# Gate spread of a sparse-expert layer: column one-hots eight tokens at a time on VectorE, gated rows divided over three engines

## Chip, cores and metric

The kernel runs on one core of one Trainium2 chip. The metric is the device time of one execution in microseconds (us); lower is better. TensorE (PE in the profile, with its weight loads as PEld), VectorE (DVE), ScalarE (ACT), GpSimd (POOL) and the DMA queue of SyncE (SP) run their own instruction streams and meet at semaphores.

## The reference, cut to what matters

The whole program is a two-direction gated linear attention mixer, a PEER layer and two further transformer layers over 512 tokens of width 1024. The change is in the PEER layer. Each token picks 128 experts (8 heads with 16 picks each) out of 128 x 128, and gives each a gate:

```python
expert = (jnp.take_along_axis(i1, top_c // PEER_TOPK, axis=-1) * PEER_N_KEYS
          + jnp.take_along_axis(i2, top_c % PEER_TOPK, axis=-1))
gate = jax.nn.softmax(top_s, axis=-1)
act = jax.nn.gelu(jnp.einsum("pd,ped->pe", xb, jnp.take(u, eb, axis=0)), approximate=False)
return jnp.einsum("pe,ped->pd", (gb * act).astype(v.dtype), jnp.take(v, eb, axis=0))
```

## The kernel before, in words

For 384 of the 512 tokens (`TD`) the kernel does not gather expert rows. It computes all 16384 experts for those tokens as dense products and multiplies by a gate matrix that is zero where an expert was not picked. (The other 128 tokens do gather their rows, later.) So each token needs a 128 x 128 matrix of gates: expert number = 128 * e1 + e2, and the gate of pick s belongs at column e2[s] and row e1[s]. The stage that makes these matrices is called the spread, and it is the only place that the change touches.

At its start the tiles `e1T`, `e2T` and `gT` (the profile calls all of them `eT`) hold e1, e2 and the gate with the 128 picks on the partitions and the 384 tokens along the free axis. `iota` is 0 to 127 along the free axis. For token t two 128 x 128 f32 tiles are made:

- `ob`: a one-hot row per pick, `iota == e2T[:, t]` (the column one-hot);
- `oa`: `(iota == e1T[:, t]) * gT[:, t]` (the gated row).

TensorE multiplies the two (L2199, two passes in f32, so 768 matmul records for 384 tokens), four tokens to a PSUM bank. ScalarE copies each full bank to `stage` (L2223, 96 copies), and after 32 tokens the DMA queue of SyncE writes a stage to `gd` in DRAM (L2257, 12 writes).

Who makes what: VectorE makes all 384 `oa` tiles (L2235) and 72 of the `ob` tiles (L2238). GpSimd makes 192 `ob` tiles with one comparison each (L2249). ScalarE makes the remaining 120 `ob` tiles with two instructions each, `|e2 - iota|` (L2215) and `relu(1 - x)` (L2217). `expert_engine(t)` fixes who makes `ob` of token t, with a period of 16 tokens: 3 on VectorE, 5 on ScalarE, 8 on GpSimd.

There are 16 buffers of each kind (`NOH`), so whoever makes a tile for token t waits for the matmul of token t - 16. Each engine goes through its own tokens in order. ScalarE's order of tiles and bank copies is `spread_order`: its tiles of tokens 4q + 8 to 4q + 11 come before the copy of bank q. The stage begins when the transposed picks have been copied out of PSUM (L2091), and the next stage (the experts) starts after all five engines have left this one.

Of the kernel before, what the change touches and what calls it, by code (L numbers as in the profile page):

```python
# [7 lines left out]
ALU = mybir.AluOpType  # L8
ACT = mybir.ActivationFunctionType
# [1668 lines left out]
TD = 384  # L1678
# [29 lines left out]
def peer_plan(k):  # L1708
    m = k.m
    k.U2 = m.pair("Up", [128, KC, TX])  # L1710
    k.own = Net()
    k.own.x = m.sb("ownx", [128, D])
    k.own.at, k.own.atf = m.sb("ownat", [128, NSLOT], U32), m.sb("ownatf", [128, NSLOT])
    k.own.gate, k.own.dot, k.own.w = (m.sb("own", [128, NSLOT]) for _ in range(3))
    own_u = m.top
    k.early = [m.sb("early", [128, 4, TD // 2]) for _ in range(5)]
    k.early += [k.X[:, c:c + 4, TX:TX + TD // 2] for c in (0, 4)]
    m.top = own_u
    k.own.u = [m.sb("ownu", [128, D]) for _ in range(NUB)]
    top = m.top  # L1720
    m.top = own_u + 10 * D
    k.n2 = NormMod(k, "n2", k.X, k.sc2, k.MOD[0][:, 24:32, :], k.U2, (XR,), sums_at=own_u, sums=4, rows=3)
    assert m.top <= top and k.n2.s.end <= own_u + 10 * D
    m.top = top
    k.peer_top = m.top
    k.iota, k.marks = m.sb("iota", [128, 128]), m.sb("marks", [128, 32])
    k.e1T, k.e2T, k.gT = (m.sb("eT", [128, TD]) for _ in range(3))
    top2 = m.top
    k.R = Retrieval(k)
    m.top = top2  # L1730
    k.oa = [m.sb("oa", [128, 128]) for _ in range(NOH)]
    k.ob = [m.sb("ob", [128, 128]) for _ in range(NOH)]
    k.stage = [m.sb("stage", [128, 128, BT]) for _ in range(2)]
    last = m.sb("early", [128, 4, TD // 2])
    assert k.R.end <= m.top
    k.early += [m.sb("early", [128, 4, TD // 2]) for _ in range(NE - 8)] + [last]
    m.top = top
    k.gt = [m.sb("gt", [128, TD // BT, 4, BT]) for _ in range(2)]
    k.acts = [m.pair("act", [128, 2, TD]) for _ in range(2)]
    k.ge = [m.sb("ge", [128, TD]) for _ in range(2)]  # L1740
    k.own.acc = k.X[:, 0:4, TX:T]
    side = m.top
    k.side = [m.sb("side", [128, TW]) for _ in range(2)]
    k.cb2 = m.sb("cb", [128, 2 * D])
    k.dots3 = Dots(k, "experts", k.cb2, k.X[:, 4:8, TX:T])
    k.own.v = [m.sb("ownv", [128, D]) for _ in range(NVB)]
    end, m.top = m.top, side
    k.ot = [m.sb("ot", [128, D]) for _ in range(3)]
    m.top = end
# [94 lines left out]
def early_pe(k, n):  # L1844

    u = view(take(k, ("u", n)), KC)
    for i in range(2):
        project(k, k.B[EARLY_BANKS[n] + i][:, 0:TD], u, KC, 128 * i, k.U2, DENSE).then_inc(
            *k.pe.inc("mm", ("u", n, i), *([("tile", u.j)] if i else [])))
# [310 lines left out]

def expert_engine(t):

    if t % 16 in (1, 5, 7, 11, 13):
        return "act"
    return "dve" if t % 16 in (3, 8, 14) else "pool"


NOH = 16  # L2170


def spread_order():

    out = [("hot", t) for t in range(8)]
    for q in range(TD // 4):
        if q + 2 < TD // 4:
            out += [("hot", t) for t in range(4 * q + 8, 4 * q + 12)]
        out.append(("group", q))
    return out  # L2180


def spread_pe(k):
    pe = k.pe
    for q in range(TD // 4):
        b = k.B[q % 8]
        pe.wait_ge("early", (8, 1))
        if q >= 8:
            pe.wait_ge("staged", q - 8)
        for i in range(4):  # L2190
            t = 4 * q + i
            pe.wait_ge("hot_a", t)
            if expert_engine(t) == "act":
                pe.wait_ge("hot_act", t)
            elif expert_engine(t) == "dve":
                pe.wait_ge("hot_dve", t)
            else:
                pe.wait_ge("hot_pool", t)
            ins = pe.e.matmul(b[:, i * 128:(i + 1) * 128], k.ob[t % NOH][:], k.oa[t % NOH][:], start=True, stop=True)  # L2199
            ins.then_inc(*pe.inc("mm", ("hot", t)))  # L2200
    pe.mark("spread")
    pe.wait_ge("staged", TD // 4 - 7)
    early_pe(k, NE - 1)


def spread_act(k):
    a = k.act
    a.after("retrieve", "pe", "dve", "pool")
    for what, t in spread_order():
        if what == "hot":  # L2210
            if expert_engine(t) == "act":
                ob = k.ob[t % NOH]
                if t >= NOH:
                    a.wait_ge("mm", ("hot", t - NOH))
                a.e.activation(ob[:], k.iota[:], ACT.Abs, bias=k.e2T[:, t:t + 1], scale=-1.0).then_inc(*a.inc("hot_act", (t, 0)))  # L2215
                a.wait_ge("hot_act", (t, 0))
                a.e.activation(ob[:], ob[:], ACT.Relu, bias=k.one[:, 0:1], scale=-1.0).then_inc(*a.inc("hot_act", t))  # L2217
        else:
            n, i0 = 4 * t // BT, 4 * t % BT
            a.wait_ge("mm", ("hot", 4 * t + 3))  # L2220
            if n >= 2:
                a.wait_ge(f"stored{n % 2}", n - 2)
            a.e.activation(k.stage[n % 2][:, :, i0:i0 + 4], k.B[t % 8].rearrange("p (t i) -> p i t", t=4), ACT.Copy).then_inc(  # L2223
                *a.inc("staged", t))
    a.mark("spread")


def spread_dve(k):
    v = k.dve
    v.after("retrieve", "pe", "act", "pool")  # L2230
    v.wait_ge("chosen", ("T", 2))
    for t in range(TD):
        if t >= NOH:
            v.wait_ge("mm", ("hot", t - NOH))
        v.e.tensor_scalar(k.oa[t % NOH][:], k.iota[:], k.e1T[:, t:t + 1], k.gT[:, t:t + 1], ALU.is_equal, ALU.mult).then_inc(  # L2235
            *v.inc("hot_a", t))
        if expert_engine(t) == "dve":
            v.e.tensor_scalar(k.ob[t % NOH][:], k.iota[:], k.e2T[:, t:t + 1], None, ALU.is_equal).then_inc(*v.inc("hot_dve", t))  # L2238
    v.mark("spread")


def spread_pool(k):
    g = k.pool
    g.after("retrieve", "pe", "act", "dve")
    for t in range(TD):
        if expert_engine(t) == "pool":
            if t >= NOH:
                g.wait_ge("mm", ("hot", t - NOH))
            g.e.tensor_scalar(k.ob[t % NOH][:], k.iota[:], k.e2T[:, t:t + 1], None, ALU.is_equal).then_inc(*g.inc("hot_pool", t))  # L2249
    g.mark("spread")  # L2250


# [1885 lines left out]
def tensor_program(k):  # L4138
# [9 lines left out]
    n2_pe(k)  # L4148
    retrieve_pe(k)
    spread_pe(k)  # L4150
    experts_pe(k)
    join_pe(k)
# [18 lines left out]
def scalar_program(k):  # L4171
# [8 lines left out]
    n2_act(k)  # L4180
    retrieve_act(k)
    spread_act(k)
    experts_act(k)
    join_act(k)
# [19 lines left out]
def vector_program(k):  # L4204
# [8 lines left out]
    n2_dve(k)  # L4213
    retrieve_dve(k)
    spread_dve(k)
    experts_dve(k)
    join_dve(k)
# [19 lines left out]
def gpsimd_program(k):  # L4237
# [9 lines left out]
    n2_pool(k)  # L4247
    retrieve_pool(k)
    spread_pool(k)
    experts_pool(k)  # L4250
    join_pool(k)
# [34 lines left out]
def make_plan(k):  # L4286
# [32 lines left out]
    assert m.top <= heads  # L4319
    m.top = base  # L4320
    peer_plan(k)
    m.top = base
    k.r64, k.r96 = m.sb("r64", [128, 128]), m.sb("r96", [128, 128])
# [247 lines left out]
```

## Time and profile before

| what | value |
|---|---|
| timed runs, median | 5397.58 us (5397.45 to 5402.66, 3 runs) |
| span of the profiled execution | 5393.7 us |
| spread stage, first `oa` to last write of a stage issued | 1306.8 to 1441.3 us of that span |
| busy over the span: PE, DVE, ACT, POOL | 91%, 57%, 36%, 22% |

The profiled execution is one run of its own; its span lies 3.9 us below the median of the timed runs, within what a time includes around the span. The busy shares are means over all stages, so they say little on this one: in the spread all four engines are busy most of the time, and the rest of the kernel is mostly TensorE's.

### The profile page before, as it was taken

Reading aid. Unit: us, or ns where it says so; the run is one execution under the profiler, and the core shown is the slowest. Engines: PE = TensorE matmul, PEld = TensorE weight load, DVE = VectorE, ACT = ScalarE, POOL = GpSimd, SP = SyncE. Lnnn points to the kernel's source line nnn. Section 1 sums busy time; section 2 is a strip of 40 time slices with the busy share of each in tenths; the row PEclk is TensorE's granted clock in tenths of the full one; section 3 lists DMA queues with packets and bytes.
Section 4 is the critical chain, followed back from the end, with each engine's and each line's share of the span. In section 5 each row is a group of like instructions: output and inputs, shape, how many; then the busy total and the mean of one; then the engine's idle time right before and its main releaser. Section 6 shows DMA issues by size and latency. Waiting matters only on the chain.

```text
span 5393.7 us, 67249 instructions
## 1 busy us (share of the span) xinstructions
PE 4930.6 (91%) x27217; PEld 4138.9 (77%) x27217; DVE 3101.0 (57%) x5380; ACT 1915.5 (36%) x2842; POOL 1206.4 (22%) x1009
## 2 busy tenths in 40 slices
PE   7998989998899999999799898989999799889999
PEld 7887877787688888887668786778888577667787
DVE  5444455589667777776442535356656534554555
ACT  3445522235733323333342424322222343343333
POOL 1111100046644555442120002100000120021000
PEclk8999989999999999999899999999999899999999
DMA  4111023422578898984101010122322101112221
GB/s 153 52 56 57 31 94 121 155 86 108 211 251 295 313 310 310 310 291 163 51 20 64 16 47 30 48 86 110 114 97 104 43 32 64 36 45 94 86 94 71
DMA packets 157155, 636.29 MB, mean 118 GB/s; under 512 B 12352, under 2 KB 62544, under 8 KB 106288
## 3 DMA queue, kind: packets, MB, share of 16 engines
q1 hardware_dynamic: 112528, 467.97, 24.5%
q0 software_dynamic: 42240, 160.88, 8.4%
q8 instruction: 217, 3.56, 0.3%
q10 hardware_dynamic: 2080, 3.15, 0.2%
q14 instruction: 90, 0.74, 0.0%
HBM read 595.25 MB, written 36.70 MB: 117 GB/s over the span
## 4 chain that ended last, share of the span: by engine, by line
PE 74%; DVE 13%; ACT 7%; issue 3%; POOL 2%; DMA 2%; DVEq 0%; ACTq 0%; POOLq 0%; SPq 0%
PE banks L261 61%; PE banks L2918 2%; PE banks L3017 1%; PE banks L2923 1%; DVE cols L2949 1%; DVE oa L2235 1%; ACT P L2967 1%; PE banks L3044 1%; PE banks L990 1%; DVE raw L527 1%; DVE prod L527 1%; PE banks L335 1%; DMA X<-ctxT_in 1%; ACT spl1H L192 1%; PE banks L382 1%
## 5 line engine op out<-in xcount | busy, mean ns | idle before, releaser
L261 PE MATMUL banks<-UH,spl1H 128*128 128x512 f32 (+1 forms) x1600 | 588.4, 368 | 37.8 <-DVE spl1L L210 9.2
L210 DVE TENSOR_TENSOR spl0L<-raw,spl0H 128x2048 fp32r<-128x2048 f32 (+2 forms) x170 | 372.9, 2193 | 401.1 <-ACT spl0H L192 372.0
L210 DVE TENSOR_TENSOR spl1L<-raw,spl1H 128x2048 fp32r<-128x2048 f32 (+2 forms) x163 | 366.3, 2247 | 405.6 <-ACT spl1H L192 380.7
L261 PE MATMUL banks<-UL,spl1H 128*128 128x512 f32 (+1 forms) x1600 | 581.6, 364 | 0.0
L261 PE MATMUL banks<-UH,spl1L 128*128 128x512 f32 (+1 forms) x1600 | 581.3, 363 | 0.0
L261 PE MATMUL banks<-UH,spl0H 128*128 128x512 f32 (+2 forms) x1184 | 432.6, 365 | 37.8 <-DVE UL L480 10.4
L192 ACT ACTIVATE spl1H<-raw 128x2048 fp32r<-128x2048 f32 (+1 forms) x170 | 313.2, 1842 | 333.7 <-PE banks L261 255.7
L192 ACT ACTIVATE spl0H<-raw 128x2048 fp32r<-128x2048 f32 (+3 forms) x171 | 306.2, 1791 | 343.5 <-PE banks L261 254.8
L261 PE MATMUL banks<-UL,spl0H 128*128 128x512 f32 (+2 forms) x1184 | 427.2, 361 | 0.0
L261 PE MATMUL banks<-UH,spl0L 128*128 128x512 f32 (+2 forms) x1184 | 426.9, 361 | 0.0
L261 PEld LDWEIGHTS banks<-UH,spl1H 128*128 128x128 f32 x1600 | 304.5, 190 | 97.5 <-issue 36.6
L261 PE MATMUL banks<-UpH,spl0H 128*128 128x384 f32 (+1 forms) x1008 | 348.9, 346 | 26.6 <-issue 21.3
L261 PE MATMUL banks<-UpL,spl0H 128*128 128x384 f32 (+1 forms) x1008 | 345.6, 343 | 0.0
L261 PE MATMUL banks<-UpH,spl0L 128*128 128x384 f32 (+1 forms) x1008 | 345.5, 343 | 0.0
L261 PEld LDWEIGHTS banks<-UH,spl1L 128*128 128x128 f32 x1600 | 304.6, 190 | 51.0
L261 PEld LDWEIGHTS banks<-UL,spl1H 128*128 128x128 f32 x1600 | 304.8, 191 | 50.1 <-issue 0.5
L261 PE MATMUL banks<-spl1H,actH 128*128 128x512 f32 x708 | 282.4, 399 | 50.0 <-issue 40.1
L2949 DVE TENSOR_REDUCE cols<-banks 128x1 f32<-128x768 f32 (+3 forms) x240 | 190.7, 795 | 189.6 <-PE banks L2923 106.0
L261 PEld LDWEIGHTS banks<-UH,spl0H 128*128 128x128 f32 (+1 forms) x1184 | 225.3, 190 | 83.5 <-issue 35.5
L261 PE MATMUL banks<-spl1L,actH 128*128 128x512 f32 x708 | 280.1, 396 | 0.0
L261 PE MATMUL banks<-spl1H,actL 128*128 128x512 f32 x708 | 279.8, 395 | 0.0
L4095 POOL TENSOR_TENSOR cv<-cv 128x768 f32<-128x768 f32 (+1 forms) x44 | 68.9, 1566 | 846.6 <-DVE cv L4061 846.6
(483 smaller groups left out, 11698.6 us busy)
## 6 DMA issues: line engine op xcount, KB each, us to landing
raw<-uT_in SPq DMA_DIRECT2D x64, 1024.0 KB
raw<-ev_in SPq DMA_DIRECT2D x64, 1024.0 KB
raw<-up_in SPq DMA_DIRECT2D x44, 1024.0 KB
raw<-ada_in SPq DMA_DIRECT2D x40, 1024.0 KB
gd<-stage SPq DMA_DIRECT2D x12, 2048.0 KB, 6.8
gt<-gd SPq DMA_DIRECT2D x32, 768.0 KB, 7.5
side<-ada_in SPq DMA_DIRECT2D x24, 1024.0 KB, 7.0
raw<-gate_in SPq DMA_DIRECT2D x24, 1024.0 KB
```

Source lines behind the costliest of these rows:

```text
L192: a.e.activation(k.spl[i % SPL].h[:, 0:w], k.raw[j % RAW][:, 0:w], ACT.Copy).then_inc(*a.inc("w_hi", j))
L210: v.e.tensor_tensor(s.l[:, 0:w], k.raw[j % RAW][:, 0:w], s.h[:, 0:w].bitcast(F32), ALU.subtract).then_inc(*v.inc("w_lo", j))
L261: ins = pe.e.matmul(out, x, y, start=start and i == 0 and j == 0, stop=stop and i == n - 1 and j == 2)
L335: ins = pe.e.matmul(s.sums[:, o:o + 1], s.sq[i % len(s.sq)][:, c * 128:(c + 1) * 128], k.ones[:, 0:1], start=(i == 0 and c == 0), stop=(j ...
L382: ins = pe.e.matmul(b[:, c * 128:(c + 1) * 128], k.ones[:], d[:, c, :], start=True, stop=True)
L527: v.e.scalar_tensor_tensor(x if r else S.out, x, 1.0, w, ALU.mult, ALU.mult, accum_out=MOD[:, 2 * t + c, r:r + 1]).then_inc(*v.inc("dot", ...
L990: ins = pe.e.matmul(o[:, c * 64:(c + 1) * 64], w.S[:, c, x * 128:(x + 1) * 128], w.qd[:, c * 64:(c + 1) * 64], start=False, stop=(c == ord ...
L2235: v.e.tensor_scalar(k.oa[t % NOH][:], k.iota[:], k.e1T[:, t:t + 1], k.gT[:, t:t + 1], ALU.is_equal, ALU.mult).then_inc(*v.inc("hot_a", t))
L2918: ins = pe.e.matmul(k.W[1 + j][:, at:at + n], Q[lo:hi, q * 128:(q + 1) * 128], K[lo:hi, k0:k0 + n], start=True, stop=True)
L2923: ins = pe.e.matmul(k.W[1 + jj][:, at:at + n], Q[lo:hi, q * 128:(q + 1) * 128], K[lo:hi, k0:k0 + n], start=True, stop=True)
L2949: v.e.reduce_max(mx, src, AX_X).then_inc(*v.inc("largest", (tag, i, j)))
L4095: g.e.tensor_tensor(va[:, 0:w], va[:, 0:w], ga[:, 0:w], ALU.mult).then_inc(*g.inc("ffn_prod", (l, j)))
```

## The change

The column one-hots `ob` are now all made on VectorE, for eight tokens (`OBT`) in one instruction: `iota` broadcast over eight tokens is compared with eight columns of `e2T` broadcast over 128. There are 48 of them, in 3 buffers of eight tokens each (`NOB`). Their first is made ahead of everything and then each one block ahead of its rows. The gated rows `oa`, which were all VectorE's, are divided by `row_engine(t)` with a period of 24 tokens: 3 on ScalarE (48 in all), 10 on GpSimd (160), 11 on VectorE (176). ScalarE's version of a gated row is `|e1 - iota|` and then `relu(gate - gate * x)`, for which it first makes the negated gates `ngT` out of PSUM. TensorE waits for the block of columns and for the row's engine; its matmuls, the bank copies and the stage writes stay.

```diff
@@ peer_plan
-    k.e1T, k.e2T, k.gT = (m.sb("eT", [128, TD]) for _ in range(3))
+    k.e1T, k.e2T, k.gT, k.ngT = (m.sb("eT", [128, TD]) for _ in range(4))
-    k.ob = [m.sb("ob", [128, 128]) for _ in range(NOH)]
+    k.ob = [m.sb("ob", [128, OBT, 128]) for _ in range(NOB)]
@@
-def expert_engine(t):
-
-    if t % 16 in (1, 5, 7, 11, 13):
-        return "act"
-    return "dve" if t % 16 in (3, 8, 14) else "pool"
-
-
-NOH = 16
+NOH = 16
+OBT = 8
+NOB = 3
+
+
+def row_engine(t):
+
+    if t % 8 == 3:
+        return "act"
+    return "pool" if t % 24 in (0, 2, 5, 7, 9, 12, 14, 16, 18, 21) else "dve"
@@ spread_act
+    a.e.activation(k.ngT[:], k.B[6][:, 0:TD], ACT.Copy, scale=-1.0).then_inc(*a.inc("hot_row_act", "minus"))
+    a.wait_ge("hot_row_act", "minus")
-                a.e.activation(ob[:], k.iota[:], ACT.Abs, bias=k.e2T[:, t:t + 1], scale=-1.0).then_inc(*a.inc("hot_act", (t, 0)))
-                a.wait_ge("hot_act", (t, 0))
-                a.e.activation(ob[:], ob[:], ACT.Relu, bias=k.one[:, 0:1], scale=-1.0).then_inc(*a.inc("hot_act", t))
+                a.e.activation(oa[:], k.iota[:], ACT.Abs, bias=k.e1T[:, t:t + 1], scale=-1.0).then_inc(*a.inc("hot_row_act", (t, 0)))
+                a.wait_ge("hot_row_act", (t, 0))
+                a.e.activation(oa[:], oa[:], ACT.Relu, bias=k.gT[:, t:t + 1], scale=k.ngT[:, t:t + 1]).then_inc(
+                    *a.inc("hot_row_act", t))
@@
+def hot_columns_dve(k, b):
+    v = k.dve
+    if b >= NOB:
+        v.wait_ge("mm", ("hot", OBT * (b - NOB) + OBT - 1))
+    e = k.e2T[:, b * OBT:(b + 1) * OBT].unsqueeze(2).to_broadcast([128, OBT, 128])
+    v.e.tensor_tensor(k.ob[b % NOB][:], k.iota[:].unsqueeze(1).to_broadcast([128, OBT, 128]), e, ALU.is_equal).then_inc(
+        *v.inc("hot_cols", b))
@@ spread_dve
+    hot_columns_dve(k, 0)
     for t in range(TD):
-        if t >= NOH:
-            v.wait_ge("mm", ("hot", t - NOH))
-        v.e.tensor_scalar(k.oa[t % NOH][:], k.iota[:], k.e1T[:, t:t + 1], k.gT[:, t:t + 1], ALU.is_equal, ALU.mult).then_inc(
-            *v.inc("hot_a", t))
-        if expert_engine(t) == "dve":
-            v.e.tensor_scalar(k.ob[t % NOH][:], k.iota[:], k.e2T[:, t:t + 1], None, ALU.is_equal).then_inc(*v.inc("hot_dve", t))
+        if t % OBT == 0 and t // OBT + 1 < TD // OBT:
+            hot_columns_dve(k, t // OBT + 1)
+        if row_engine(t) == "dve":
+            if t >= NOH:
+                v.wait_ge("mm", ("hot", t - NOH))
+            v.e.tensor_scalar(k.oa[t % NOH][:], k.iota[:], k.e1T[:, t:t + 1], k.gT[:, t:t + 1], ALU.is_equal, ALU.mult).then_inc(
+                *v.inc("hot_row_dve", t))
@@ spread_pool
-        if expert_engine(t) == "pool":
+        if row_engine(t) == "pool":
             if t >= NOH:
                 g.wait_ge("mm", ("hot", t - NOH))
-            g.e.tensor_scalar(k.ob[t % NOH][:], k.iota[:], k.e2T[:, t:t + 1], None, ALU.is_equal).then_inc(*g.inc("hot_pool", t))
+            g.e.tensor_scalar(k.oa[t % NOH][:], k.iota[:], k.e1T[:, t:t + 1], k.gT[:, t:t + 1], ALU.is_equal, ALU.mult).then_inc(
+                *g.inc("hot_row_pool", t))
```

VectorE at the start of the spread, before the change: after the three copies out of PSUM come runs of `oa` with an `ob` now and then.

```order
L2091 COPY eT<-banks 128x384 x3
L2235 TENSOR_SCALAR oa<-iota,eT 128x128 x4
L2238 TENSOR_SCALAR ob<-iota,eT 128x128
L2235 TENSOR_SCALAR oa<-iota,eT 128x128 x5
L2238 TENSOR_SCALAR ob<-iota,eT 128x128
L2235 TENSOR_SCALAR oa<-iota,eT 128x128 x6
```

The same place of the same engine with the change: two blocks of columns come first, then three or four rows between blocks.

```order
L2091 COPY eT<-banks 128x384 x3
L2238 TENSOR_TENSOR ob<-iota,eT 128x1024 x2
L2253 TENSOR_SCALAR oa<-iota,eT 128x128 x3
L2238 TENSOR_TENSOR ob<-iota,eT 128x1024
L2253 TENSOR_SCALAR oa<-iota,eT 128x128 x4
L2238 TENSOR_TENSOR ob<-iota,eT 128x1024
L2253 TENSOR_SCALAR oa<-iota,eT 128x128 x4
```

What moved on VectorE: 72 single comparisons and 208 of its 384 rows are gone, and 48 instructions of 1024 elements stand in their place.

ScalarE at the start of the spread, before the change.

```order
L2215 ACTIVATE ob<-iota,eT 128x128
L2217 ACTIVATE ob<-ob,one 128x128
L2215 ACTIVATE ob<-iota,eT 128x128
L2217 ACTIVATE ob<-ob,one 128x128
L2223 ACTIVATE stage<-banks 128x128x4
L2215 ACTIVATE ob<-iota,eT 128x128
L2217 ACTIVATE ob<-ob,one 128x128
L2223 ACTIVATE stage<-banks 128x128x4
```

The same place with the change: the negated gates first, then one pair for every two bank copies.

```order
L2211 ACTIVATE eT<-banks 128x384
L2219 ACTIVATE oa<-iota,eT 128x128
L2221 ACTIVATE oa<-oa,eT 128x128
L2219 ACTIVATE oa<-iota,eT 128x128
L2221 ACTIVATE oa<-oa,eT 128x128
L2228 ACTIVATE stage<-banks 128x128x4 x2
L2219 ACTIVATE oa<-iota,eT 128x128
L2221 ACTIVATE oa<-oa,eT 128x128
L2228 ACTIVATE stage<-banks 128x128x4 x2
```

What moved on ScalarE: 120 pairs became 48, and one copy of 384 elements stands ahead of its first row. On GpSimd nothing changes its place: 192 single comparisons become 160 comparisons with a multiplication, in one unbroken run.

## Rows read from the trace of the kernel before

**Rows 1.** The page: busy time of each engine over the span.

```profile
span 5393.7 us, 67249 instructions
PE 4930.6 (91%) x27217; PEld 4138.9 (77%) x27217; DVE 3101.0 (57%) x5380; ACT 1915.5 (36%) x2842; POOL 1206.4 (22%) x1009
```

**Rows 2.** Chain that ended last, 1306.8 to 1441.3 us: shares by engine and line.

```profile
by line: DVE oa L2235 53.2%; PE banks L2199 10.8%; ACT stage L2223 10.2%; ACT ob L2217 9.3%; DVE ob L2238 7.5%; ACT ob L2215 6.9%; DMA gd<-stage 4.6%; issue 2.0%
```

**Rows 3.** Three stretches of the spread: start:end, length, busy us of each engine (instructions).

```profile
1306.80:1354.00 47.20, 40.82 (x271) 35.20 (x271) 47.19 (x176) 45.29 (x118) 45.99 (x75) 0.94 0.32 135
1354.00:1435.50 81.50, 69.78 (x469) 58.00 (x470) 74.84 (x281) 79.13 (x206) 73.22 (x118) 1.00 0.47 196
1435.50:1441.30 5.80, 5.08 (x35) 4.43 (x36) 0.22 (x1) 5.55 (x15) 0.36 (x1) 1.00 0.38 161
```

**Rows 4.** Groups of instructions, 1306.8 to 1441.3 us: busy us, mean ns, idle before.

```profile
L2249 POOL TENSOR_SCALAR ob<-iota,eT 128x128 f32<-128x128 f32 x192 | 119.6, 639 | 15.6 <-PE banks L2199 8.4 <-DVE eT L2091 6.1
L2223 ACT ACTIVATE stage<-banks 128x512 f32<-128x512 f32 x96 | 55.5, 579 | 0.6 <-PE banks L2199 0.4
```

**Rows 5.** Timeline of ScalarE, 1358.3 to 1361.1 us: start, length, instruction.

```profile
1358.27 0.40 ACT L2217 ACTIVATE ob<-ob,one 128x128 f32<-128x128 f32 x1
1358.58 0.39 ACT L2215 ACTIVATE ob<-iota,eT 128x128 f32<-128x128 f32 x1
1359.00 0.40 ACT L2217 ACTIVATE ob<-ob,one 128x128 f32<-128x128 f32 x1
1359.31 0.58 ACT L2223 ACTIVATE stage<-banks 128x512 f32<-128x512 f32 x1
1359.78 0.39 ACT L2215 ACTIVATE ob<-iota,eT 128x128 f32<-128x128 f32 x1
```

**Rows 6.** Timeline of TensorE at 1340 us, and its L2199 with durations.

```profile
1340.15 0.72 PE L2199 MATMUL banks<-oa,ob 128*128 128x128 f32 x5
...
L2199 PE MATMUL banks<-oa,ob x768: 274/275/552, 1307.7 to 1440.4; 128*128 128x128 f32 x192
```

**Rows 7.** Timeline of VectorE, a 1024-element comparison (L2000) behind a 2048-element subtraction.

```profile
1163.04 2.28 DVE L210 TENSOR_TENSOR spl0L<-raw,spl0H 128x2048 fp32r<-128x2048 f32 x1
1165.23 1.22 DVE L2000 TENSOR_TENSOR ge<-small,marks 128x1024 f32<-128x1024 f32 x1
1166.37 0.87 DVE L1942 MAX8 vals<-sc 128x8 f32<-128x128 f32 x4
```

**Rows 8.** Timeline of GpSimd in those microseconds, and one undisturbed such instruction (groups, 1270 to 1275 us).

```profile
1163.30 3.31 POOL L2139 TENSOR_TENSOR cand<-vals 128x64 f32<-128x64 f32 x1 [0.83 <-DVE topc L1953]
...
L2139 POOL TENSOR_TENSOR cand<-vals 128x64 f32<-128x64 f32 x1 | 0.3, 302 | 0.8 <-DVE topc L1953 0.8
```

**Rows 9.** Timelines of GpSimd and VectorE at 1296 us: both start within 0.06 us.

```profile
1296.17 4.56 POOL L224 TENSOR_TENSOR spl0L<-raw,spl0H 128x2048 fp32r<-128x2048 f32 x1 [7.82 <-issue]
...
1296.23 5.58 DVE L2040 TENSOR_TENSOR eq<-eq,small 128x1024 f32<-128x1024 f32 x1
```

**Rows 10.** Timelines of GpSimd and VectorE in the spread, single instructions.

```profile
1309.41 0.71 POOL L2249 TENSOR_SCALAR ob<-iota,eT 128x128 f32<-128x128 f32 x1
1310.11 0.60 POOL L2249 TENSOR_SCALAR ob<-iota,eT 128x128 f32<-128x128 f32 x1
1310.68 0.60 POOL L2249 TENSOR_SCALAR ob<-iota,eT 128x128 f32<-128x128 f32 x1
...
1309.45 0.28 DVE L2238 TENSOR_SCALAR ob<-iota,eT 128x128 f32<-128x128 f32 x1
1309.90 0.33 DVE L2235 TENSOR_SCALAR oa<-iota,eT 128x128 f32<-128x128 f32 x1
1310.16 0.39 DVE L2235 TENSOR_SCALAR oa<-iota,eT 128x128 f32<-128x128 f32 x1
```

**Rows 11.** GpSimd scalar instructions elsewhere: durations (min/median/max ns), two operations (L1164), one (L873).

```profile
L1164 POOL TENSOR_SCALAR k<-lg x16: 833/838/842, 96.1 to 419.6; 128x768 f32<-128x768 f32 x16
L873 POOL TENSOR_SCALAR kd<-b x24: 922/926/929, 114.5 to 679.5; 128x256 f32<-128x256 f32 x24
```

More of the change, by code:

```diff
@@ L2191, in spread_pe @@
             t = 4 * q + i
[L2192 to L2196, printed above, removed]
-            else:
-                pe.wait_ge("hot_pool", t)
-            ins = pe.e.matmul(b[:, i * 128:(i + 1) * 128], k.ob[t % NOH][:], k.oa[t % NOH][:], start=True, stop=True)
+            pe.wait_ge("hot_cols", t // OBT)
+            if row_engine(t) == "act":
+                pe.wait_ge("hot_row_act", t)
+            elif row_engine(t) == "dve":
+                pe.wait_ge("hot_row_dve", t)
+            else:
+                pe.wait_ge("hot_row_pool", t)
+            ins = pe.e.matmul(b[:, i * 128:(i + 1) * 128], k.ob[t // OBT % NOB][:, t % OBT, :], k.oa[t % NOH][:], start=True, stop=True)
             ins.then_inc(*pe.inc("mm", ("hot", t)))
@@ L2208, in spread_act @@
     a.after("retrieve", "pe", "dve", "pool")
+    a.e.activation(k.ngT[:], k.B[6][:, 0:TD], ACT.Copy, scale=-1.0).then_inc(*a.inc("hot_row_act", "minus"))
+    a.wait_ge("hot_row_act", "minus")
     for what, t in spread_order():
         if what == "hot":
-            if expert_engine(t) == "act":
-                ob = k.ob[t % NOH]
+            if row_engine(t) == "act":
+                oa = k.oa[t % NOH]
                 if t >= NOH:
                     a.wait_ge("mm", ("hot", t - NOH))
-                a.e.activation(ob[:], k.iota[:], ACT.Abs, bias=k.e2T[:, t:t + 1], scale=-1.0).then_inc(*a.inc("hot_act", (t, 0)))
-                a.wait_ge("hot_act", (t, 0))
-                a.e.activation(ob[:], ob[:], ACT.Relu, bias=k.one[:, 0:1], scale=-1.0).then_inc(*a.inc("hot_act", t))
+                a.e.activation(oa[:], k.iota[:], ACT.Abs, bias=k.e1T[:, t:t + 1], scale=-1.0).then_inc(*a.inc("hot_row_act", (t, 0)))
+                a.wait_ge("hot_row_act", (t, 0))
+                a.e.activation(oa[:], oa[:], ACT.Relu, bias=k.gT[:, t:t + 1], scale=k.ngT[:, t:t + 1]).then_inc(
+                    *a.inc("hot_row_act", t))
         else:
```

## Prediction, made before the changed kernel ran

> **What bounds the kernel now.** I read the page first: TensorE is busy 91% of the span, GpSimd 22% [rows 1]. That mean says nothing on the spread, so I took the chain of the stage next. There TensorE has 11%; rows and columns made on VectorE have 61%, ScalarE's three lines 26% [rows 2]. The stage lasts 134.5 us and lies wholly on the chain.
>
> Busy time by stretch shows who sets the pace [rows 3]. Until 1354 us VectorE is busy 47.19 of 47.20 us. From then to 1435.5 us ScalarE is (79.13 of 81.50), VectorE has gaps (74.84), and for the last 5.8 us ScalarE finishes alone. ScalarE's own pace follows from its timeline [rows 5]: a pair takes 0.42 + 0.31 = 0.73 us from start to start, a bank copy 0.47. For 120 pairs and 96 copies that is 120 x 0.73 + 96 x 0.47 = 132.7 us, the length of the stage. VectorE runs 176 instructions in the first 47.2 us, 0.268 us each, so 456 of them need 122 us. GpSimd starts one in 47.20 / 75 = 0.63 us, 192 x 0.63 = 121 us; it is busy for 119.6 of the 134.5 us, and the 96 bank copies of ScalarE waited for TensorE 0.4 us in all [rows 4]. TensorE, when fed, needs (0.72 - 0.275) / 4 = 0.111 us per matmul record [rows 6], so 768 x 0.111 = 85.5 us: the floor of this stage. So three engines stand close together at 121 to 133 us, and the change can give up to 49 us, if no engine takes over the place of the slowest.
>
> **The change part by part.** ScalarE: 48 pairs and 96 copies, 48 x 0.73 + 96 x 0.47 = 80.2 us, plus one copy of 384 elements at the start, about 0.5 us. A scale read per partition in the second of a pair isn't in the trace; even 0.1 us more is 5 us of a slack of 50. ScalarE leaves the path.
>
> VectorE: 176 rows x 0.268 = 47.2 us. The 48 blocks of columns have a close relative in the trace: a comparison of 1024 elements with both inputs broadcast takes 1.22 us, 1.14 from its start to the next start [rows 7]. 48 x 1.14 = 54.7 us. Sum 101.9 us without waits, against 122 before.
>
> GpSimd: 160 instructions instead of 192. An undisturbed one takes 0.60 us and the next starts 0.57 to 0.58 after it [rows 10]; with fewer VectorE rows in its way I take 0.60 per row, 96 us in all. The new form has a second operation and a second value per partition. L1164 does two operations on 768 elements in 0.84 us, while L873, one operation with a value per partition, takes 0.93 us for 256 [rows 11]: the second operation is cheap, the value read per partition is what costs. Bounds for the second value: nothing, or the work per element once more. From 128 elements at 0.60 us and 256 at 0.926, an element costs 2.5 ns, so once more is 0.32 us, 51 us over 160 rows. I take nothing, since one tile of values more is not one pass more, and keep part of it as a rival.
>
> These three sums alone would give 102 us. But a price stands in the trace that the diff doesn't show: **VectorE instructions with two SBUF inputs and GpSimd instructions exclude each other.** At 1296 us a GpSimd subtraction starts 0.06 us ahead of a VectorE product of 1024 elements [rows 9]. GpSimd ends at 1300.73; VectorE's 1.22 us become 5.58 and end at 1301.81, 1.08 us after it. So VectorE asks 0.14 us after its start and then holds for 1.08. The other way round, GpSimd's 0.30 us instruction starts at 1163.30 inside a VectorE subtraction, and a broadcast comparison follows that until 1166.45. It ends at 1166.61, after 3.31 us [rows 7, 8]. It too asks some 0.14 us in. That comparison is of the form of the new columns, so broadcasting does not exempt them.
>
> The Trainium skill ("SBUF — State Buffer", section "Who interferes with whom") says the same: a VectorE instruction with two SBUF inputs contends with a GpSimd instruction that reads SBUF. It adds that whoever comes first keeps the port pair for its whole instruction. The pairs of rows above agree. In the spread it is otherwise for GpSimd's scalar form. Within one GpSimd instruction (1309.41, 0.71 us) one VectorE comparison starts at 1309.45 and takes 0.28, and the rows after it go on [rows 10]. One side pays 0.1 at most: GpSimd 0.71 instead of 0.60, or VectorE 0.39 instead of 0.33 at 1310.16. So that form keeps the other out for about 0.1 us of its 0.60, from 0.14 to 0.25 after its start (1310.16 + 0.14 + 0.06 is 0.25 after 1310.11).
>
> What does a block of columns then cost GpSimd? An instruction under way past its 0.25 us finishes; the next waits at its 0.14 until the hold of 1.08 ends. The delay is 1.08 less the time from VectorE's grant to GpSimd's next request. With GpSimd the slowest, VectorE waits in its queue for a matmul, and TensorE for GpSimd's row. Let a GpSimd row end at 0: the matmul pair ends near 0.49 (0.1 + 0.11 + 0.28), VectorE starts 0.04 later and is granted at 0.67, while GpSimd would ask at 0.70 and, another row on, at 1.28. The block's wait is on tokens 7, 15 and 23 of 24, which lie 0, 1 and 2 tokens (0.22 us each) behind the last GpSimd row. Grants at 0.67, 0.89 and 1.11 cost GpSimd 1.05, 0.69 and 0.91 us, mean 0.88. 48 x 0.88 = 42 us. Bounds: 0.6 (a grant just after GpSimd's window) and 1.08 (the whole hold each time), 29 to 52 us.
>
> **The sum.** GpSimd is the bound: 96 + 42 = 138 us, plus 1.2 us behind its last row (matmul 0.5, bank copy 0.6), 139.4 us against 134.5: +5 us. VectorE, with 102 us and some tenths of waiting per block, has room and hides in it; so do ScalarE (80) and TensorE (85.5). At the start TensorE gets its first pair about 1 us later than before, since the columns come first; that lies within GpSimd's sum, which counts its wait on the first block. Behind the stage all is as before: stage write, then the loads of the experts, and any shift goes through one to one. The span of 5393.7 becomes 5398.6, and as the median lay 3.9 us above the span, 5397.6 + 5 = **5402.5 us**. With the bounds of the delay (29 and 52 us for 42) it is 5389 to 5412.
>
> **The rivals.**
> (a) GpSimd isn't held up: its port need falls between VectorE's holds, or VectorE is the one that waits and briefly. For it: GpSimd's own window is short. Against: 3.31 us for 0.30 [rows 8]. VectorE then bounds, 101.9 plus 1.2 ahead of its first row and 1.2 behind the last, 104.5 us: 30 us less, 5368 us. If VectorE pays 0.3 us for each block, 14 us more, 5382. It decides once the delay per block is below 0.55 us: then GpSimd needs less than 123 us.
> (b) GpSimd keeps the pair for its whole instruction in this form too. Then the next one asks just behind VectorE's grant, each block costs the full 1.08, and 96 + 52 + 1.2 gives 149 us: +15, 5412 us. Against it stand the undisturbed VectorE rows of [rows 10]; for it, [rows 9]. The skill's rule named above is this case.
> (c) The second value per partition costs GpSimd 0.1 us a row (a third of the bound): +16 us on the forecast, 5418 us. It decides from 0.04 us a row, where it passes the band of no change.
> (d) The change does not relieve ScalarE, because its row instructions with a scale per partition take much longer. To matter they must rise by over 1 us each: no row speaks for it.
>
> **Chances.** The forecast's mechanism 0.46, with its own range 5389 to 5410; (a) 0.22; (b) 0.15; (c) 0.17; (d) under 0.01. A measurement of this kernel tells about 0.2% (10.8 us) from no change, so 5386.8 to 5408.4 is "same". Of the forecast's 0.46, 0.03 falls below that band and 0.03 above. (a) is faster. (b) and (c) are slower. Faster 0.25, same 0.40, slower 0.35. A range from 5368 to 5420 leaves out about half of (a) and half of (c), 0.2 in all.
>
> **What the new profile would show.** Right: GpSimd busy without a gap in the spread, with about 48 of its 160 rows lengthened to 1.2 to 1.7 us and the others at 0.60; VectorE's column blocks at 1.2 to 1.3 us and gaps before its rows that end with TensorE; ScalarE busy about 60% of the stage, with gaps. If (a), GpSimd's rows all stay near 0.6 and VectorE has no gaps, the stage takes 105 to 120 us. If (b), column blocks of 1.2 to 1.7 us and a stage near 149. If (c), the shortest GpSimd rows stand well above 0.60 us. The prediction is wrong if the chain of the stage goes through TensorE's own pace or ScalarE, neither of which I expect, or if what the stage gains is taken back by the loads that follow it.

## The result, and the profile after

The changed kernel takes 5435.4 us (median of 4 runs) against 5397.5 us: slower by 37.9 us, a ratio of 1.007 (95% interval 1.0058 to 1.0082). The forecast was 5402.5 us with a range up to 5420, so both the number and the range missed.

The chain of the spread stage after, shares by line (for [rows 2]):

```profile
by line: POOL oa L2265 76.6%; PE banks L2201 22.0%; DMA gd<-stage 4.0%; issue 1.0%; ACT stage L2228 0.3%
```

Three stretches of the stage (for [rows 3]): start:end, length, then busy us of PE, PEld, DVE, ACT and POOL with their instructions:

```profile
1306.00:1354.00 48.00, 33.62 (x201) 27.59 (x202) 30.51 (x63) 24.90 (x53) 47.99 (x43) 0.91 0.21 88
1354.00:1474.00 120.00, 86.94 (x536) 69.27 (x536) 74.35 (x162) 63.81 (x134) 120.00 (x113) 0.99 0.38 158
1474.00:1480.20 6.20, 5.94 (x39) 5.08 (x40) 0.49 (x2) 3.71 (x8) 4.52 (x6) 1.00 0.01 3
```

And the groups of the stage (for [rows 4]): busy us, mean ns, idle before and who ended it:

```profile
L2265 POOL TENSOR_SCALAR oa<-iota,eT 128x128 f32<-128x128 f32 x160 | 172.5, 1093 | 6.2 <-DVE eT L2091 6.2
L2201 PE MATMUL banks<-oa,ob 128*128 128x128 f32 x768 | 125.8, 301 | 48.5 <-POOL oa L2265 44.2
L2238 DVE TENSOR_TENSOR ob<-iota,eT 128x1024 f32<-128x1024 f32 x48 | 59.3, 1236 | 63.3 <-PE banks L2201 63.1
L2228 ACT ACTIVATE stage<-banks 128x512 f32<-128x512 f32 x96 | 57.0, 594 | 80.1 <-PE banks L2201 80.0
```

GpSimd is busy without a gap from the first row to the last, 172.5 us; its one wait is for the stage to begin. Before, VectorE and then ScalarE were the full ones; now each has gaps that end with TensorE, and TensorE waits for GpSimd. The stage takes 174.2 us (1306.0 to 1480.2) instead of 134.5, 39.7 us more. The profiled span grew by 44.6 us and the timed median by 37.9, so the stage holds what the kernel lost. The other 5 us between the two profiled spans lie outside the stage; the profiled execution was the slowest of the four (5439.6 us), and the medians don't show them.

Durations of one line (min/median/max ns) and single instructions from the timelines of GpSimd and VectorE (for [rows 9, 10]):

```profile
L2265 POOL TENSOR_SCALAR oa<-iota,eT x160: 786/838/2884, 1306.0 to 1477.7; 128x128 f32<-128x128 f32 x160
L2238 DVE TENSOR_TENSOR ob<-iota,eT x48: 1210/1237/1254, 1305.9 to 1471.0; 128x1024 f32<-128x1024 f32 x48
...
1320.30 0.79 POOL L2265 TENSOR_SCALAR oa<-iota,eT 128x128 f32<-128x128 f32 x1
1321.08 1.50 POOL L2265 TENSOR_SCALAR oa<-iota,eT 128x128 f32<-128x128 f32 x1
1320.57 1.25 DVE L2238 TENSOR_TENSOR ob<-iota,eT 128x1024 f32<-128x1024 f32 x1 [1.72 <-PE banks L2201]
```

Two things are to be seen. No GpSimd row is shorter than 0.786 us, where the forecast took 0.60. And there is a wait between the two engines: the block of columns that starts in the middle of a GpSimd row (0.27 us into it) takes its usual 1.25 us, while the next GpSimd row, started at 1321.08, ends at 1322.58, 0.76 us after the block: it waited for the block's end. VectorE hardly waits (its longest block is 1.254 us), GpSimd does.

If the block starts only 0.04 us into a GpSimd row, that very row is held:

```profile
1338.35 1.87 POOL L2265 TENSOR_SCALAR oa<-iota,eT 128x128 f32<-128x128 f32 x1
1338.39 1.24 DVE L2238 TENSOR_TENSOR ob<-iota,eT 128x1024 f32<-128x1024 f32 x1 [1.38 <-PE banks L2201]
```

In all, 47 of the 160 GpSimd rows take over 1.1 us. Nearly all of them belong to one of three kinds: 15 take 1.50 us, 13 take 1.80 and 14 take 1.86 to 1.87.

So two costs stand side by side: a dearer row, and a wait of GpSimd for VectorE's block, which the prediction put down to a shared SBUF port. The experiments take them apart.

### The profile page after: what moved, and what is told of

Its sections match the earlier page's. It is cut to its first block, busy times and chain, and to the rows that moved or that the text cites. A ratio compares the mean times of both kernels' runs of the same rounds, so it can differ in the third digit from the quotient of the medians.

```text
span 5438.3 us, 66550 instructions
## 1 busy us (share of the span) xinstructions
PE 4948.4 (91%) x27217; PEld 4149.4 (76%) x27217; DVE 3083.2 (57%) x5148; ACT 1877.0 (35%) x2699; POOL 1255.6 (23%) x977
## 4 chain that ended last, share of the span: by engine, by line
PE 73%; DVE 11%; ACT 6%; POOL 5%; issue 3%; DMA 2%; DVEq 0%; ACTq 0%; POOLq 0%; SPq 0%
PE banks L261 61%; POOL oa L2265 2%; PE banks L2935 2%; PE banks L2940 1%; PE banks L3034 1%; DVE cols L2966 1%; ACT P L2984 1%; PE banks L3061 1%; PE banks L990 1%; DVE raw L527 1%; DVE prod L527 1%; PE banks L335 1%; PE banks L382 1%; ACT spl1H L192 1%; DMA X<-ctxT_in 1%
```

## The experiments

**1. Four forms of GpSimd's row in one kernel.** By groups of 24 tokens, each form on a line of its own (names shortened, the semaphore updates left out):

```diff
+            f = t // 24 % 4
+            if f == 0:
+                g.e.tensor_scalar(oa, iota, e1T[t], None, is_equal)          # L2267
+            elif f == 1:
+                g.e.tensor_scalar(oa, iota, e1T[t], 1.0, is_equal, mult)     # L2269
+            elif f == 2:
+                g.e.tensor_scalar(oa, iota, 3.0, 1.0, is_equal, mult)        # L2271
+            else:
+                g.e.tensor_scalar(oa, iota, e1T[t], gT[t], is_equal, mult)   # L2273
```

> GpSimd's rows are made in four forms, changing every 24 tokens: one comparison with a value per partition; the same and a multiplication by the constant 1; comparison and multiplication with constants only; comparison and multiplication with two values per partition, as in the change. The gates are left out of the first three, so three quarters of GpSimd's rows are ungated. Theory A (the second value per partition is what a row pays for): undisturbed durations of about 0.60, 0.60, below 0.60 and 0.79 us. Theory B (the second operation costs): 0.60, 0.79, and 0.79 us for the last. Theory C (the 0.79 us comes from the stage: port contention with VectorE's column blocks, whatever the form): all four near 0.79 us.

GpSimd's durations by line (min/median/max ns):

```profile
L2267 POOL TENSOR_SCALAR oa<-iota,eT x40: 590/596/2698, 1307.4 to 1427.9; 128x128 f32<-128x128 f32 x40
L2269 POOL TENSOR_SCALAR oa<-iota,eT x40: 707/737/1715, 1317.9 to 1437.4; 128x128 f32<-128x128 f32 x40
L2271 POOL TENSOR_SCALAR oa<-iota x40: 634/637/1564, 1327.3 to 1445.7; 128x128 f32<-128x128 f32 x40
L2273 POOL TENSOR_SCALAR oa<-iota,eT x40: 778/852/1861, 1335.6 to 1454.9; 128x128 f32<-128x128 f32 x40
```

The minima are the undisturbed ones. All forms stood in the same stage beside the same kind of blocks, and their minima differ, so theory C falls. Theories A and B are each right in part: the second operation adds 0.117 us (0.590 to 0.707), and a value per partition in place of its constant adds 0.071 (to 0.778). The kernel was timed once, 5408.8 us, which lies between the times of the dear and the cheap row, as it should; no more is read from it.

The prediction had taken the price of the second operation from wide rows. The kernel before has a GpSimd row of 768 elements with one operation and a value per partition:

```profile
L3002 POOL TENSOR_SCALAR P<-P,cols 128x768 f32<-128x768 f32 x32 | 70.6, 2206 | 95.4 <-DVE cols L2985 95.4
```

That is 2.206 us against 0.838 for two operations on constants (L1164 in [rows 11]). At 128 elements the order is reversed: 0.590 us for one operation with a value, 0.634 for two on constants. So the two wide lines of [rows 11] could not give the price of a row of 128.

**2. GpSimd's rows as one comparison, all else as changed.**

```diff
-            g.e.tensor_scalar(k.oa[t % NOH][:], k.iota[:], k.e1T[:, t:t + 1], k.gT[:, t:t + 1], ALU.is_equal, ALU.mult)
+            g.e.tensor_scalar(k.oa[t % NOH][:], k.iota[:], k.e1T[:, t:t + 1], None, ALU.is_equal)
```

> The changed kernel, but every GpSimd row is one comparison with e1 alone; the gate is left out of GpSimd's 160 rows. Theory A or B (the form costs 0.19 us a row): GpSimd needs 160 x 0.58 + 48 blocks x 0.95 + 3 = 141 us, the stage takes 143 us instead of 174, the kernel about 5404 us, which is what was forecast for the change. Theory C (port contention makes the 0.79 us): the stage stays above 165 us and the kernel above 5425 us.

Measured 5402.3 us, ratio to the kernel before 1.0009 (0.9999 to 1.0018). GpSimd's group:

```profile
L2265 POOL TENSOR_SCALAR oa<-iota,eT 128x128 f32<-128x128 f32 x160 | 137.5, 878 | 6.1 <-DVE eT L2091 6.1
```

This kernel is the one that the prediction costed: rows of 0.60 us and the port's price. GpSimd was reckoned at 138 us and took 137.5; the stage at 139.4, and it took 139.3 (1306.6 to 1445.9); the kernel at 5402.5. The port term was right, the row term was not: with the gate the same 160 rows keep GpSimd busy for 35.0 us more.

**3. Column blocks that read e2 from PSUM.** They have one SBUF input then. The race for the port is gone with the input, not with a wait; TensorE has seven banks in turn instead of eight.

```diff
@@ banks; ScalarE's copies use the same list, and the wait behind the stage is put at TD // 4 - 4 (not shown)
+HOTB = (0, 1, 2, 3, 4, 6, 7)
@@ spread_pe
-        b = k.B[q % 8]
-        if q >= 8:
-            pe.wait_ge("staged", q - 8)
+        b = k.B[HOTB[q % 7]]
+        if q >= 7:
+            pe.wait_ge("staged", q - 7)
@@ hot_columns_dve (the broadcast at the end of the line is left out here)
-    e = k.e2T[:, b * OBT:(b + 1) * OBT].unsqueeze(2)
+    e = k.B[5][:, b * OBT:(b + 1) * OBT].unsqueeze(2)
```

> The changed kernel, but the column blocks read e2 from the PSUM bank in which the transposes leave it, instead of its copy in SBUF, so they have one SBUF input; the matmuls use the seven other banks in turn. If blocks of columns hold GpSimd up over the SBUF port: no GpSimd row is lengthened any more, 160 x 0.775 + 3 = 127 us, stage 128 us, the kernel about 5390 us. If the 48 long GpSimd rows come from something else (waits for matmuls, the ring of 16 buffers), the stage stays near 174 us and the kernel near 5435 us. If VectorE's blocks become much longer with an input in PSUM (over 1.6 us), VectorE bounds at 125 us or more.

Measured 5394.3 us, ratio 0.9992 (0.9982 to 1.0001). GpSimd's group and durations, and the new blocks:

```profile
L2266 POOL TENSOR_SCALAR oa<-iota,eT 128x128 f32<-128x128 f32 x160 | 128.5, 815 | 6.2 <-DVE eT L2091 6.2
...
L2266 POOL TENSOR_SCALAR oa<-iota,eT x160: 774/787/948, 1308.5 to 1436.2; 128x128 f32<-128x128 f32 x160
L2239 DVE TENSOR_TENSOR ob<-iota,banks x48: 1206/1221/1223, 1308.4 to 1430.0; 128x1024 f32<-128x1024 f32 x48
```

The longest GpSimd row falls from 2884 to 948 ns, and its sum from 172.5 to 128.5 us. So the second SBUF input of the blocks cost GpSimd 44.0 us, 0.92 us for each of 48. The blocks themselves do not take longer with an input in PSUM (median 1221 ns against 1237), and the shortest row is still 774 ns, so the dearer row is not a matter of this wait.

**4. Both off.** Edits 2 and 3 together.

> Both costs taken off the changed kernel at once: column blocks read e2 from PSUM, and GpSimd's 160 rows are one comparison without the gate (the gate is left out of these rows). If the two costs are all that the change lost, the sums without them hold: GpSimd 160 x 0.58 + 3 = 96 us, VectorE 102 us, stage about 105 us, kernel about 5368 us, some 30 us below the one before. Rival: a further cost stands behind them (VectorE's rows held up by GpSimd's, or ScalarE's bank copies, for which TensorE waited in the last experiments): stage 115 us or more, kernel 5380 us or more.

Measured 5370.6 us, ratio 0.9953 (0.9936 to 0.9969). GpSimd:

```profile
L2266 POOL TENSOR_SCALAR oa<-iota,eT 128x128 f32<-128x128 f32 x160 | 94.6, 610 | 13.9 <-PE banks L2202 7.6 <-DVE eT L2091 6.1
```

The four kernels make a table of GpSimd's busy time: 172.5 (both), 137.5 (port only), 128.5 (dear row only), 94.6 (neither). Each cost is nearly the same with and without the other: the port 44.0 and 42.9 us, the row 35.0 and 33.9. In GpSimd's busy time they add. In the kernel's time they don't quite: taking off the row alone gives 33 us, the port alone 41, both 65 and not 74. With both off GpSimd has gaps (7.6 us of waiting for TensorE), and VectorE's two lines hold 90% of the stage's chain. The rival cost behind them, for which the kernel had to stay at 5380 us or more, isn't there.

**5. Blocks of four tokens.** `OBT = 4`, `NOB = 6`; as many column values, in twice as many instructions.

> The changed kernel with blocks of four tokens in six buffers: 96 column blocks of 512 elements instead of 48 of 1024. A block holds the port for half as long (about 0.55 us, as a two-input instruction of 512 elements takes 0.69 us in all). If GpSimd loses the hold less the 0.13 us that it loses less than the hold now (0.95 of 1.08), a block costs 0.42 us and 96 of them 40 us: GpSimd 124 + 3 + 40 = 167 us, stage 169, kernel about 5430 us. If each block costs a fixed time (0.95 us, a hand-over and not the hold), 91 us: stage 220 us, kernel about 5481 us.

Measured 5435.7 us, ratio 1.0073 (1.0057 to 1.009), the same as the change.

```profile
L2265 POOL TENSOR_SCALAR oa<-iota,eT 128x128 f32<-128x128 f32 x160 | 173.6, 1099 | 6.2 <-DVE eT L2091 6.2
L2238 DVE TENSOR_TENSOR ob<-iota,eT 128x512 f32<-128x512 f32 x96 | 65.8, 686 | 13.4 <-PE banks L2201 13.2
```

GpSimd loses 173.6 - 128.5 = 45.1 us over 96 blocks, 0.47 us each, half of 0.92. The rival of a fixed time per block falls (it asked for 220 us). Against the 0.42 us expected it is 0.05 more a block, which is 5 of the 6 us between 5430 and the measured time. In these two sizes what GpSimd loses follows the length of VectorE's instruction.

**6. Another division of the rows, columns as changed.** `row_engine` gives 6 of 24 rows to GpSimd, 4 to ScalarE, 14 to VectorE.

> The changed kernel with the rows divided otherwise in 24 tokens: 6 on GpSimd (was 10), 4 on ScalarE (was 3), 14 on VectorE (was 11). If the cost of the change is GpSimd's sum alone: 96 rows x 0.775 + 48 x 0.95 = 120 us, VectorE 48 x 1.15 + 224 x 0.268 = 115 us, ScalarE 64 x 0.81 + 96 x 0.5 = 100 us, so a stage of 122 us and a kernel about 12 us below the one before, 5385 us. Rival: with three engines so close, each waits for the others through the rings, the stage takes 130 us or more and the gain on the kernel before is below 5 us.

Measured 5388.3 us, ratio 0.9984 (0.9974 to 0.9993). The chain of its stage:

```profile
by line: POOL oa L2265 95.9%; PE banks L2201 3.0%; ACT stage L2228 0.5%; DVE eT L2091 0.5%; issue 0.3%; PE banks L1836 0.2%; POOLq L97 0.0%
```

GpSimd is still the bound with 96 rows, busy 123.2 us where 120 were reckoned: 46 us of port for 77 of rows. The gain of 9 us lies between the rival's 5 and the expected 12, but the rival's mechanism isn't what is missing: the chain runs through GpSimd almost without a break, so waits for the other engines did not slow it. Its own sum came out 3 us longer than reckoned.

**7 and 8. e2 from PSUM, and 8 of 24 rows on GpSimd.** With 4 on ScalarE and 12 on VectorE:

```diff
-    if t % 8 == 3:
+    if t % 6 == 3:
         return "act"
-    return "pool" if t % 24 in (0, 2, 5, 7, 9, 12, 14, 16, 18, 21) else "dve"
+    return "pool" if t % 3 == 2 else "dve"
```

> All outputs full: e2 read from PSUM, and of 24 rows 8 on GpSimd, 4 on ScalarE, 12 on VectorE. GpSimd 128 x 0.775 + 2 = 101 us, VectorE 48 x 1.14 + 192 x 0.268 = 106 us, ScalarE 64 x 0.81 + 96 x 0.5 = 100 us: stage about 109 us, kernel about 5372 us. Rival: with ScalarE this full its bank copies come late and TensorE waits for banks, of which there is one less: stage 118 us or more, kernel 5381 us or more.

With 3 on ScalarE and 13 on VectorE (edit not shown):

> The same with 8 rows on GpSimd, 3 on ScalarE, 13 on VectorE. VectorE 48 x 1.14 + 208 x 0.268 = 110 us is the longest sum, ScalarE has 48 x 0.81 + 96 x 0.5 = 87 us: stage 113 us, kernel about 5376 us, 4 us above the version with 4 rows on ScalarE. If late bank copies are what limits, it is the faster of the two.

Measured 5369.6 us, ratio 0.9952 (0.9935 to 0.9969), and 5377.6 us, ratio 0.9966 (0.9953 to 0.9978). The order is the expected one, with 8 us between them instead of 4, so late bank copies don't decide. The first is the fastest version with full outputs: 28 us below the kernel before, 66 below the change. Its middle stretch and its chain:

```profile
1354.00:1412.00 58.00, 52.66 (x423) 48.98 (x423) 58.00 (x133) 55.04 (x124) 58.00 (x71) 1.00 0.57 241
...
by line: DVE ob L2239 45.0%; DVE oa L2254 44.8%; PE banks L2202 8.5%; PE banks L1836 0.6%; ACT stage L2229 0.6%; DVE eT L2091 0.5%; issue 0.4%; DVEq L83 0.0%
```

VectorE and GpSimd are both busy for all 58.00 us, ScalarE for 55.04, TensorE for 52.66: another division of the rows has little left to give.

## Why the prediction was wrong, by its own steps

**What bounds the kernel before, and the sums of VectorE and ScalarE**, hold as far as the runs test them. Experiment 4 shows the three sums without the port's price: 102 us and "30 us less, 5368 us" were said, 5370.6 us was measured with VectorE as the bound. A scale per partition lengthens ScalarE's second instruction from 0.40 to 0.49 us, within the 0.1 us allowed, and ScalarE left the path as said.

**The step that failed is GpSimd's row.** "[T]he second operation is cheap, the value read per partition is what costs" came from two lines of other shapes and other operations [rows 11], and "I take nothing" for the second value was a choice that no row bore out. Side by side in one stage the second operation costs 0.117 us and the second value 0.071, together 0.19 us. The term "0.60 per row, 96 us in all" is 128.5 us when measured without the port (experiment 3), 32.5 us more. That alone makes 5402.5 into 5435. Rival (c) had the smaller part of it, the second value, at 0.1 us a row where it costs 0.071; the larger part, the second operation, was in no rival. The range ended at 5420, hardly above rival (c), although the text had a bound of 0.32 us a row. With 160 instructions on the bounding engine a tenth of a microsecond each is 16 us, more than the 10.8 us by which the prediction could tell a change from none, so this unknown should have set the width of the range.

**The port** was right in kind and size. 0.88 us per block was worked out from the time at which TensorE frees VectorE; 0.92 and 0.89 were measured (44.0 and 42.9 us over 48), 42 us forecast. The agreement is no luck of the mean, for the three cases behind it are there too. The forecast gave delays of 1.05, 0.91 and 0.69 us; in experiment 2, where a row is 0.60 us, 14 rows take 1.65, 15 take 1.58 and 15 take 1.35 to 1.36: delays of 1.05, 0.98 and 0.75. One detail doesn't fit. The delay of 1.05 falls on a row that has begun 0.02 us before the block, and if both engines ask 0.14 us after their start, as the prediction had it, GpSimd would have been first. At what moment this form asks stays open. Rival (a), that GpSimd isn't held up, falls with experiment 3; experiment 4 shows the time that it would have given, had the rows been cheap as well.

**Who waits.** Rival (b) was the one place where the rows and the Trainium skill differed. The Trainium skill ("SBUF — State Buffer", "SBUF: two separate sides", and for the exclusive lock also "Who interferes with whom") says that whoever starts first keeps the pair for the whole instruction. The trace of the change disagrees for GpSimd's small scalar form. The block at 1320.57 began 0.27 us into a GpSimd row of 0.79 us, and would have needed over 1.5 us had it waited for the row's end; it took 1.25, and none of the 48 took more than 1.254. The stage of experiment 2 says the same, 139.3 us where rival (b) asks for 149. The prediction had argued this from VectorE rows with one SBUF tensor as input [rows 10]; it is the blocks, with two, that show it. In the other direction the Trainium skill's rule holds: GpSimd waits for the end of VectorE's two-input instruction, and half the length of it costs half (experiment 5). With one input in PSUM there is no such wait in 48 blocks, as the Trainium skill has it ("SBUF — State Buffer", "Who interferes with whom") for VectorE instructions with at most one SBUF input outside the two-port modes.

**What the new profile would show**: GpSimd without a gap, 47 lengthened rows for about 48, gaps on VectorE and ScalarE all came (the lengthened ones at 1.5 to 1.87 us, since the rows themselves were longer); "the others at 0.60" did not, and the sign named for (c), shortest rows well above 0.60 us, is what stands there.

## What to carry to other kernels

Before work is moved to GpSimd, measure the very form and width that it will run there: one more operation and one more value per partition made a row of 128 elements 0.19 us longer, and 160 of them undid a stage. When VectorE gets a wide instruction with two SBUF inputs beside a busy GpSimd, count its full length once more on GpSimd's side, or let one of its inputs stay in PSUM. And divide work by measured totals per engine: here the same change with one input left in PSUM and two rows of 24 fewer on GpSimd is 66 us faster.

## What the runs showed of the hardware

- GpSimd, 128 x 128 f32, shortest durations: comparison with one value per partition 0.590 us, two operations on constants 0.634, with one value and one constant 0.707, with two values 0.774 to 0.787 from run to run.
- A broadcast comparison of 1024 elements on VectorE takes 1.21 us at least with both inputs in SBUF and 1.206 with one in PSUM.
- With its rows back to back, GpSimd loses 0.92 us to each such instruction of 1024 elements with two SBUF inputs, nothing with one of them in PSUM, and 0.47 us to each of 512 elements with two SBUF inputs, while VectorE's blocks lose under 0.05 us to GpSimd's small rows in the changed kernel and 0.15 at most in experiment 1 (1.360 us against 1.211).
